# The mixer's variance is stored and rooted earlier in each turn

## The reference, cut to what matters

```
kk = heads(zk * k_k)
kk = kk / max(sqrt(sum(kk * kk, axis=-1)), 1e-12)      # the key's factor
...
_, y = scan(step, s0, (r, decay, k, v, -kk, kk * a))
mu  = mean(y, axis=-1)
var = mean(square(y - mu), axis=-1)
y = (y - mu) * rsqrt(var + GN_EPS)                      # the output's factor
y = y * ln_w + ln_b + bonus
merged = sigmoid(gate_a) * attention + sigmoid(gate_b) * (y * g)
```

## Time and profile before

| | us |
|---|---|
| median of 3 runs | 2990.63 |
| the runs | 2985.22, 2990.63, 2991.81 |
| the profiled execution | 2991.62 |
| its span | 2989.5 |
| TensorE busy in it | 2911.4 |
| VectorE busy | 1559.7 |
| ScalarE busy | 1113.2 |
| GpSimd busy | 1280.0 |

### The profile page before, as it was taken

How to read it: one execution, slowest core, us unless ns; L and a number is a source line. 1 busy time by engine, 2 the same in 40 slices (tenths; PEclk the granted TensorE clock), 3 DMA queues, 4 the chain that set the end, 5 groups by cost and what they waited for, 6 DMA issues and landing times. The chain is left out here.

```text
span 2989.5 us, 62088 instructions
## 1 busy us (share of the span) xinstructions
PE 2911.4 (97%) x27008; PEld 2391.5 (80%) x27008; DVE 1559.7 (52%) x1823; ACT 1113.2 (37%) x1841; POOL 1280.0 (43%) x674
## 2 busy tenths in 40 slices
PE   7999999999999999999999999999999999999998
PEld 6888888888778877877877787877778888888887
DVE  6544444543366566656566666445335844443443
ACT  5333334333334433333444444333233433333342
POOL 2444446462455444444454555232130344445451
PEclk9999999999999999999999999999999999999999
DMA  6222236344321111131111122362013322225442
GB/s 194 80 81 82 85 113 238 109 142 162 102 60 57 50 50 50 39 116 50 50 50 50 52 63 77 102 191 65 28 57 120 102 85 82 78 81 200 170 148 64
DMA packets 286314, 282.04 MB, mean 94 GB/s; under 512 B 14176, under 2 KB 236640, under 8 KB 284896
## 3 DMA queue, kind: packets, MB, share of 16 engines
q1 hardware_dynamic: 286048, 278.12, 28.8%
HBM read 227.75 MB, written 50.33 MB: 93 GB/s over the span
## 5 line engine op out<-in xcount | busy, mean ns | idle before, releaser
L1713 POOL TENSOR_TENSOR panels_low<-arena,panels_high 128x1024 fp32r<-128x1024 f32 x103 | 249.9, 2426 | 387.5 <-ACT panels_high L2118 380.0
L671 POOL TENSOR_TENSOR panels_low<-arena,panels_high 128x1024 fp32r<-128x1024 f32 x97 | 241.8, 2492 | 323.4 <-ACT panels_high L855 323.4
L1825 PE MATMUL bank<-half_high,panels_high 128*128 128x512 f32 (+1 forms) x896 | 355.7, 397 | 9.0 <-DMA half_low<-h_spill 4.7
L1825 PE MATMUL bank<-half_low,panels_high 128*128 128x512 f32 (+1 forms) x896 | 340.7, 380 | 0.0
L1825 PE MATMUL bank<-half_high,panels_low 128*128 128x512 f32 (+1 forms) x896 | 339.4, 379 | 0.0
L1825 PEld LDWEIGHTS bank<-half_high,panels_high 128*128 128x128 f32 x896 | 169.2, 189 | 60.7 <-issue 19.6
L1966 PE MATMUL bank<-arena 64*64 64x64 f32 x5120 | 214.0, 226 | 0.7 <-issue 0.3
L771 PE MATMUL bank<-h_high,panels_high 128*128 128x512 f32 x528 | 205.4, 389 | 0.0
L771 PE MATMUL bank<-h_low,panels_high 128*128 128x512 f32 x528 | 205.4, 389 | 0.0
L771 PE MATMUL bank<-h_high,panels_low 128*128 128x512 f32 x528 | 205.4, 389 | 0.0
L1067 DVE TENSOR_TENSOR ffn_work<-bank,ffn_work 128x512 f32<-128x512 f32 x80 | 54.9, 688 | 284.7 <-ACT ffn_work L914 194.6
(11 more groups left out here) (407 smaller groups left out, 7641.7 us busy)
## 6 DMA issues: line engine op xcount, KB each, us to landing
arena<-w_in SPq DMA_DIRECT2D x96, 512.0 KB, 3.8
arena<-w_down SPq DMA_DIRECT2D x88, 512.0 KB, 4.1
a_spill<-ffn_work SPq DMA_DIRECT2D x88, 256.0 KB, 2.0
arena<-a_spill SPq DMA_DIRECT2D x88, 256.0 KB, 2.8
arena<-w_gate SPq DMA_DIRECT2D x19, 1024.0 KB, 5.6
arena<-w_up SPq DMA_DIRECT2D x19, 1024.0 KB, 8.0
arena<-w_ckv SPq DMA_DIRECT2D x16, 512.0 KB, 4.9
bridge<-w_out SPq DMA_DIRECT2D x14, 512.0 KB, 5.0
```

Source lines behind the costliest of these rows:

```text
L671: nc.gpsimd.tensor_tensor(low, src, high.bitcast(F32), ALU.subtract).then_inc(s_low, 1)
L1713: G.tensor_tensor(pw[1][:, unit % 2], raw[unit % 2], pw[0][:, unit % 2].bitcast(F32), ALU.subtract).then_inc(S("panel_low"), 1)
L1825: last = mm(dst, pw[wp][:, unit % 2, kt], src, start=term == 0, stop=term == TERMS - 1)
```

## The change

In every turn that is both `live` and `out`, from 2 to 15, GpSimd takes the variance's power before the two operations on the chunk ends, behind a new wait on `kk_spread` of the same turn (since `root` is read by the spreading of the key's factor until then). Turn 15 had this order already and gets the wait. In turns 16 and 17 the place is the one of before. In turns 2 to 14 VectorE stores the variance right behind the spreading of the key's factor (L2308), ahead of L2360 and L2362, where it had come behind them.

```diff
@@ GpSimd, prepare(i) @@
-                        if i == ITER - 1:
+                        if live and out:
+                            pool.wait_ge(S("kk_spread"), i + 1)
                             root_var()
                         if live:
                             pool.wait_ge(S("decay_ready"), 2 * i + 1)
@@
                             G.tensor_copy(pend[i % 2].unsqueeze(2), ends).then_inc(S("ends_ready"), 1)
                             G.tensor_tensor(ar[i % 2][:, :, 2, :], over_chunks(c("stack_ident")),
                                             ends.broadcast_to([P, NC, CH]), ALU.mult).then_inc(S("ends_ready"), 1)
-                        if out and i != ITER - 1:
+                        if out and not live:
                             root_var()
                         for j in range(2, NP - 1):
                             next_panel(i, j)
@@ VectorE, prepare(i) @@
                             if i < ITER - 1:
                                 spread_kk()
+                            if out and i < ITER - 1:
+                                store_var()
                             V.tensor_tensor(cur[:, :, 1, :], by_chunk(rm), by_chunk(pin), ALU.mult).then_inc(
                                 S("rows_ready"), 1)
                             V.scalar_tensor_tensor(out=t1[:], in0=rm[:], scalar=par_of("r_k", p), in1=kp[:],
                                                    op0=ALU.mult, op1=ALU.mult).then_inc(S("rk_ready"), 1)
-                            if out and i < ITER - 1:
-                                store_var()
                             seen("kk_unscaled")
```

## The result

The changed kernel takes 2991.48 us (median of 22 runs), the kernel before 2987.36 us (median of 22, of which the three shown above are part). The ratio is 1.0014, 95% interval 1.0008 to 1.002, so the change costs 4.1 us (2.4 to 6.0). The prediction's 2994.7 us stood on the median of the first three runs, 2990.63 us, which lies 3.3 us above that of all 22; the change itself is what its sum forecast. The profiled execution after took 2996.84 us (span 2994.7), which is 5.4 us above the median of its kernel: the profile is read for its parts, not for its total.

What follows compares the result with a forecast made beforehand. TensorE, busy 97%, bounds the kernel, so only its waits count: 12 turns x 0.34 us = +4.1 us on the median 2990.63 gives 2994.7 us. Forecast's own range 2991 to 2998 us; with the faster rival, 2981 to 2999 us.

Steps and rivals of the forecast that it cites:

- the prediction's last part: Expected profile after: TensorE's wait on the variance's copy grows from 0.50 to about 0.84 us a turn, 8.3 to 12.4 us.
- Steps 1 and 2: VectorE's 0.15 us store moves at no cost under the first panel; GpSimd's power ends at 1231.57, 2.1 us earlier.
- Steps 3 and 4: VectorE runs on without the store; GpSimd's chunk-end product is held by L2373 and ends 0.93 us after it, at 1233.60.
- Step 5: VectorE's L2377 is held because the chunk-end product L1764 has waited longer; it ends at 1234.15.
- Step 6: GpSimd's second panel goes before VectorE's variance copy L2390, which ends at 1236.69 against 1236.35 before.
- Step 7: TensorE's transpose L1913 moves with the copy, +0.34 us in each of 12 turns; nothing behind gives it back.
- The copy ahead of the panel: Rival: VectorE's variance copy ends before the second panel, TensorE's wait goes, 12 x 0.72 = -8.6 us, 2982.0; chance 0.17.
- The held store: Rival: the store waits under the first panel and delays VectorE 0.15 us more; 12 x 0.49 = +5.9 us, 2996.5; chance 0.12.
- The power that holds VectorE for its whole length: Rival: GpSimd's power L1755 holds VectorE's L2362 until 1231.57; +1.14 us a turn, +13.7 us, 3004.3; chance 0.03.
- Reading (c): When a VectorE or GpSimd operation ends and both have something ready, the waiting engine goes and the one just finished is held.
- slower by over 0.2%: Whole-kernel outcome given 0.18: half the held store, the power holding VectorE, and an eighth of the forecast for scatter.

Runs made afterwards that it cites:

- e3: Kernel before plus one GpSimd wait on var_spread ahead of the second panel in turns 2 to 14; ratio 0.9966 to the kernel before, -10.2 us.
- e5: Whole change plus GpSimd's wait on var_spread ahead of the second panel in turns 2 to 14; ratio 0.997 to the kernel before, -9.0 us.
- e2: Changed kernel with the store back in its old place, so only the power is early; ratio 0.9967 to the kernel before, median 2977.68 us.
- e4: Changed kernel plus a useless second 8-column copy of the chunk ends on GpSimd, turns 2 to 15; ratio 0.9969 to the kernel before, -9.3 us.
- e6: Changed kernel with the second panel ahead of the chunk ends in turns 2 to 14, no new wait; ratio 1.0012 to the kernel before, +3.6 us.

## Why the prediction was right

- **What bounds it.** TensorE's 0.50 us wait at the transpose in 12 turns was the only place where the change could show, and it was: 8.3 us of waits became 12.4 us, as the prediction's last part said. That it fits to the tenth is partly luck: turn 15, which has no part in the sum, gave 0.1 us of it.
- **Steps 1 and 2.** Right. The store took 0.15 us and L2363 still ended right behind the first panel; the power ended at 1231.58 in the times of before (1234.30 - 2.72), forecast 1231.57.
- **Steps 3 and 4.** Right. The product ended 0.91 us after L2374's end (1236.31 against 1235.40), forecast 0.93; it came in behind the second of the three two-input operations.
- **Step 5.** L2378 was held 1.55 us; it ended at 1234.14 in the times of before, forecast 1234.15.
- **Step 6.** The panel went before the copy, which ended at 1236.66 in the times of before, forecast 1236.69. Four runs let the copy go ahead of the panel, by a wait (e3, e5), by a later store (e2) and by one more copy (e4), and the wait of the 12 turns is gone each time; e6 swaps product and panel and the gap stays at 0.83 us.
- **Step 7.** 0.32 us a turn in TensorE's gap, 0.33 us in the length of a turn; forecast 0.34. +4.1 us forecast, +4.1 us measured. The mechanism carries the size, but agreement to the tenth is luck where the interval is 2.4 to 6.0 us. The measured median, 2991.48 us, is near the lower end of the forecast's own range (2991 to 2998), because the three runs that it started from were 3.3 us high.
- **The rivals.** The copy ahead of the panel did not happen here but is real: e2 and e4 make it, at -9.9 and -9.3 us (forecast -8.6, inside both intervals), and the order turns near where the prediction had put it, at L2377's start: with the product starting 0.50 us ahead of it (after) the kernel is slow, 0.11 and 0.09 us behind it (e2, e4) it is fast. The held store: its row is 0.15 us long (1229.92), so the store was not held. It runs from 0.08 us before the key's spreading ends to 0.07 us after, so it slips in at the boundary at which the waiting panel takes over; the rows don't show what a store would do in the middle of a panel. The power that holds VectorE for its whole length: L2365 took 0.74 us beside it, as without it in the kernel before, so it did not.
- **Reading (c), who goes next.** The prediction had three boundaries for it. In the rows of the mixer in all nine profiles, VectorE's 512-column operations with no PSUM operand began during one of GpSimd's long operations (a panel, the product of the probabilities or that of the chunk ends) 748 times, the last 0.1 us of a row left out, the nearest only 0.05 us behind GpSimd's start, and each ended 0.27 to 0.57 us after GpSimd's end. The other way, such a GpSimd operation began during one of VectorE's 538 times, the nearest 0.06 us behind, and each ended at least 0.91 us after VectorE's end. There is no exception. The Trainium skill's rule ("SBUF — State Buffer", Who interferes with whom) of an exclusive lock for the whole instruction fits these long operations, and does not fit the power of 8 columns, whose row is 2.09 us long while L2365 runs beside it in 0.74 us.
- **A slip in the chances.** The parts that the prediction names for "slower by over 0.2%" add up to 0.17, not 0.18 (0.06 + 0.03 + an eighth of 0.62).

## What to carry to other kernels

A step that is ready earlier gains nothing if what it releases stands in a queue behind something else, so look first at how long the released instruction's own row is: a 2.60 us copy that takes 0.41 us elsewhere is waiting inside its row, and the list of waits does not show it. When VectorE and GpSimd work on SBUF side by side, write down the order of their boundaries before moving anything by half a microsecond; each move changes which operation is caught. If one short VectorE operation feeds the bounding engine, let the long GpSimd operation wait for it with a semaphore (-10 us here for one wait), rather than hope that it comes out ahead.

## What the runs showed that I had not expected

That the order is so exact a function of start times. From the product to the copy, the start times of the 12 turns repeat to 0.02 us in each profile. Moving the start of one GpSimd product from 0.50 us ahead of a VectorE operation to 0.1 us behind it takes some 1.0 us off each turn, 13 to 14 us off the kernel, in a direction that neither the amount of work nor the idle time of GpSimd suggests; the counts above put the point at which the order turns within about 0.06 us of the two starts being equal. And that, in the one pair of kernels that tries it, the order of the GpSimd operations ahead of VectorE's copy does not count: product then panel (after) and panel then product (e6) leave TensorE with the same gap, 0.82 and 0.83 us.
